# A two-layer hybrid decoder trunk on one core: the opening rebuilt, two closings and the halves of w_up moved, and 20 transposes of the identity on PE before the first tile

## The reference

```
for l in range(2):
    h = rmsnorm(x, norm_mix)
    q_a, k_a, v_a, q_b, k_b, v_b, z, xbc, dt_raw = split_cols(h @ w_in, IN_SIZES)
    q_a, k_a = apply_rope(q_a, positions), apply_rope(k_a, positions)
    y_a = swa_sink_attention(q_a, k_a, v_a, swa_sinks)        # 8 heads, window 128
    y_b = moba_attention(q_b, k_b, v_b)                       # 8 heads
    y_c = ssd_mixer(z, xbc, dt_raw, conv_w, conv_b, dt_bias, a_log, d_skip, ssd_norm)
    g_a, g_b, g_c = jnp.split(sigmoid(h @ w_gate + b_gate), 3, axis=-1)
    x = x + (g_a * (y_a @ w_br_swa) + g_b * (y_b @ w_br_moba) + g_c * (y_c @ w_br_ssd)) @ w_mix_out
    x = x + CrossAttn(rmsnorm(x, norm_cross), rmsnorm(mem, norm_mem))
    x = x + jnp.square(jax.nn.relu(rmsnorm(x, norm_mlp) @ w_up)) @ w_down
return rmsnorm(x, final_norm)
```

## Time and profile before

| what | value |
|---|---|
| median of 3 runs | 1207.43 us |
| the profiled execution's own time | 1205.99 us |
| its span | 1204.2 us |
| PE busy | 1168.9 us (97%) |
| DVE busy | 774.5 us (64%) |
| ACT busy | 573.3 us (48%) |
| POOL busy | 66.1 us (5%) |
| loads | 199.04 MB read, 166 GB/s over the span |

### The profile page before, as it was taken

One profiled execution on the slowest core, in us unless ns is written; L12 is line 12 of the kernel. 1 busy time (PEld: TensorE's weight loads), 2 busy tenths in 40 slices (PEclk: granted clock), 3 DMA queues, 4 the chain that ended last, 5 costly groups with the idle time before them and its releaser, 6 DMA issues. The chain is left out here.

```text
span 1204.2 us, 18337 instructions
## 1 busy us (share of the span) xinstructions
PE 1168.9 (97%) x7503; PEld 1047.6 (87%) x7503; DVE 774.5 (64%) x1172; ACT 573.3 (48%) x808; POOL 66.1 (5%) x93
## 2 busy tenths in 40 slices
PE   4999999999999999999999999999999999999997
PEld 3998899999998887888889888999989988888886
DVE  5877765886654456656568677568685445655655
ACT  5545454534554355344355545544455444534443
POOL 2000001410000000000000000043000000000000
PEclk9999999999999999999999999999999999999999
DMA  5743525746643445655636533366655443575560
GB/s 183 229 156 110 171 71 179 232 137 218 199 165 133 154 148 188 210 175 176 209 109 209 175 126 120 112 186 193 204 182 190 152 148 105 175 243 168 190 220 36
DMA packets 156412, 201.31 MB, mean 167 GB/s; under 512 B 7152, under 2 KB 111912, under 8 KB 156328
## 3 DMA queue, kind: packets, MB, share of 16 engines
q1 hardware_dynamic: 155296, 199.46, 51.0%
q10 hardware_dynamic: 1032, 0.67, 0.2%
HBM read 199.04 MB, written 1.08 MB: 166 GB/s over the span
## 5 line engine op out<-in xcount | busy, mean ns | idle before, releaser
L1401 DVE TENSOR_TENSOR w_lo<-raw,w_hi 128x2048 fp32r<-128x2048 f32 (+1 forms) x184 | 412.5, 2245 | 249.6 <-ACT w_hi L742 249.5
L742 ACT ACTIVATE w_hi<-raw 128x2048 fp32r<-128x2048 f32 (+1 forms) x184 | 343.2, 1875 | 108.4 <-PE psum L1114 78.5
L1097 PE MATMUL psum<-act_both,w_hi 128*128 128x256 f32 x832 | 240.9, 290 | 0.0
L1099 PE MATMUL psum<-act_both,w_lo 128*128 128x256 f32 x832 | 235.2, 283 | 0.0
L1098 PE MATMUL psum<-act_both,w_hi 128*128 128x256 f32 x832 | 235.2, 283 | 0.0
L1085 PE MATMUL psum<-act_both,w_hi 128*128 128x512 f32 x512 | 181.8, 399 | 2.3 <-DVE w_lo L1401 2.3
L1097 PEld LDWEIGHTS psum<-act_both,w_hi 128*128 128x128 f32 x832 | 159.3, 191 | 1.1 <-issue 0.5
L1098 PEld LDWEIGHTS psum<-act_both,w_hi 128*128 128x128 f32 x832 | 159.4, 192 | 0.6 <-issue 0.5
L1099 PEld LDWEIGHTS psum<-act_both,w_lo 128*128 128x128 f32 x832 | 159.2, 191 | 0.0
L1086 PE MATMUL psum<-act_both,w_lo 128*128 128x256 f32 x512 | 143.5, 280 | 0.0
L1085 PEld LDWEIGHTS psum<-act_both,w_hi 128*128 128x128 f32 x512 | 96.1, 188 | 27.2 <-DVE w_lo L1401 3.1
(11 more groups left out here) (252 smaller groups left out, 1923.9 us busy)
## 6 DMA issues: line engine op xcount, KB each, us to landing
raw<-in_w_in_dram SPq DMA_DIRECT2D x35, 1024.0 KB, 5.0
raw<-in_w_up_dram SPq DMA_DIRECT2D x32, 1024.0 KB, 5.4
raw<-in_w_down_dram SPq DMA_DIRECT2D x32, 1024.0 KB, 4.9
raw<-in_w_gate_dram SPq DMA_DIRECT2D x24, 1024.0 KB, 7.1
raw<-in_w_ckv_dram SPq DMA_DIRECT2D x16, 1024.0 KB, 5.2
raw<-in_w_br_ssd_dram SPq DMA_DIRECT2D x8, 1024.0 KB, 10.0
raw<-in_w_mix_out_dram SPq DMA_DIRECT2D x8, 1024.0 KB, 5.0
raw<-in_w_cq_dram SPq DMA_DIRECT2D x8, 1024.0 KB, 5.3
```

The source lines that it names most:

```text
L742: act.activation(w_hi[:, slot, 0:n], raw[:, slot, 0:n], ACT.Copy).then_inc(hi_ready.sem, 1)
L1097: pe.matmul(dst, m_hi[:, k, cs], a_hi[:, k, :], start=k == 0, stop=False)
L1099: ins = pe.matmul(dst, m_lo[:, k, cs], a_hi[:, k, :], start=False, stop=k == kt - 1)
L1401: dve.tensor_tensor(w_lo[:, slot, 0:n], raw[:, slot, 0:n], w_hi[:, slot, 0:n].bitcast(F32), ALU.subtract).then_inc(lo_ready.sem, 1)
```

## The change

**Opening, layer 0.** SP loads both x tiles first, then units 0 and 1 in halves, unit 2, the seven parameter rows (moved from ACT's queue), the four parameters by heads, unit 3. ACT issues three loads, squares two values of a constant (`mark_act`), squares both x tiles, and then splits units 0 and 1 by halves, with a bank of activations between any two (`hi_half`, `norm_gain_hi`). DVE scales both tiles, and alternates `lo_half` and `norm_gain_lo` likewise; the rope angles (`sine_angles`) move behind unit 3's `lo`. PE makes each half unit of a tile in blocks: all hi x hi, then hi x lo, then lo x hi (`opening`), in the order (unit, tile) = (0,0), (0,1), (1,0), (1,1); `rows_turn` stands before the last. Ahead of it all PE makes 20 transposes of the identity into bank 3, which nobody reads.

**Opening, layer 1.** The order stays (0,0), (1,0), (0,1), (1,1), in blocks as above; unit 1 is split in halves, tile 1's transposes stand around the second half of (1,0), and `norm_gain_lo` of bank 2 comes before `lo` of unit 2.

**Middle.** `ACS_SLOT` one slot later. Closing 1 one slot later. Closing 6 from behind unit 33 into the middle of unit 34. `yoff` from YB to SB. `xs_tokens` reads tile 1 first.

**w_up.** `relu_hi` moves behind the split of unit u+3 (`relu_high`); the third norm's squares move to slot U_UP+4 and write their waste to `xdec`.

The diff, cut to its core:

```
-ACS_SLOT, BTOK_SLOT, CB_SLOT, STATES_SLOT = U_XBC[3] + 1, U_XBC[4] + 3, U_XBC[5] + 4, U_XBC[5] + 6
+ACS_SLOT, BTOK_SLOT, CB_SLOT, STATES_SLOT = U_XBC[3] + 2, U_XBC[4] + 3, U_XBC[5] + 4, U_XBC[5] + 6
-TURN_SLOT = [s + (2 if i < 3 else 1) for i, s in enumerate(CLOSE_SLOT)]
+INNER_CLOSINGS, OUTER_CLOSINGS = (0, 1, 2, 6), (3, 4, 5, 7)
+TURN_SLOT = [s + (3 if i == 1 else 2 if i in INNER_CLOSINGS else 1) for i, s in enumerate(CLOSE_SLOT)]
...
         if branch == 2 and tile == 1 and s == CLOSE_SLOT[i]:
-            out.append((YB_, ("yoff", group)))
+            out.append((SB_, ("yoff", group)))
...
                     if l == 0 and u == RING:
+                        for name, r0, n in (("norm_cross", 8, 8), ("norm_mem", 16, 8), ("norm_mlp", 24, 8),
+                                            ("ssd_norm", PC_SSDN, 8), ("conv_b", PC_CONVB, 12),
+                                            ("b_gate", PC_BGATE, 24)):
+                            sp.dma_start(rows[r0:r0 + n, :, :], a[name].rearrange("l (k p) -> k l p", p=P))\
+                              .then_inc(par_loaded, 16)
...
+                    if (l, u) == (0, 0):
+                        for t in range(TT):
+                            sp.dma_start(x_sb[:, t, :], a["x"][0, t * P:(t + 1) * P, :]).then_inc(x_loaded[t], 16)
+                    if l == 0 and u < 2:
+                        sp.dma_start(dst[:, 0:2, :], src[:, 0:2, w["col"]:w["col"] + n])\
+                          .then_inc((raw_first, raw_second)[u], 16)
...
+            act.wait_ge(lo_ready.sem, RING)
+            act.activation(mark_act[:], pool_c[:, 0, :], ACT.Square)
...
                     ins.then_inc(up_lo.sem, 1)
-                    act.wait_ge(*relu_sq.at(l, j + 1))
-                    act.activation(relu_hi[:, (j // 2) % 2, 2 * (j % 2):2 * (j % 2) + 2, :], two(pT_sb[:, j % 2, :]),
-                                   ACT.Copy).then_inc(relu_h.sem, 1)
                     return
...
                     if u + RING < NU and w["kind"] != "xbc":
                         hi(l, u + RING)
+                    if (l, u) == (0, U_QA + 1):
+                        sines()
+                    if w["kind"] == "up":
+                        relu_high(l, w["index"])
...
-                    if u == NORM_TURN_SLOT[2] or u == U_CO + 3:
+                    if u == NORM_TURN_SLOT[2] or u == U_UP + 4:
...
+            for _ in range(20):
+                pe.transpose(psum[:, 3, 0:P], ident[:], ident[:])
...
+            def opening(l, u, t):
...
+                pe.wait_ge(*norm_hi.at(l, 2 * t + u + 1))
+                for ks in ((0, 1), (2, 3)) if t == 0 else (range(4),):
...
+                    for k in ks:
+                        pe.matmul(dst, act_hi[:, 4 * u + k, ts], m_hi[:, k, :], start=u == 0 and k == 0, stop=False)
+                    if last:
+                        wait_lo(pe, l, u)
+                    else:
+                        pe.wait_ge(*(lo_first, lo_second)[u].at(l, 1))
+                    for k in ks:
+                        pe.matmul(dst, act_hi[:, 4 * u + k, ts], m_lo[:, k, :], start=False, stop=False)
+                    pe.wait_ge(*is_read(l, ("norm", 0, 2 * t + u)))
+                    for k in ks:
+                        ins = pe.matmul(dst, act_lo[:, 4 * u + k, ts], m_hi[:, k, :], start=False,
+                                        stop=u == 1 and k == 3)
+                    if (u, t) == (l > 0, 0) and not last:
+                        norm0_turn(l, 1, (0,))
+                if (u, t) == (l > 0, 0):
+                    norm0_turn(l, 1, (1,))
...
                         if (l, u) == (0, 2):
-                            pe.wait_ge(cols_ready, 1)
+                            pe.wait_ge(cols_turned, 2)
...
-                for t in range(TT):
+                for t in (1, 0):
                     key = ("xs", g, t)
```

More of the change, by code:

```diff
@@ L833, in evacuate, with relu_high @@
                     ins.then_inc(free((u, 0)), 1)
+            def relu_high(l, j):
+                act.wait_ge(*relu_sq.at(l, j + 1))
+                act.activation(relu_hi[:, (j // 2) % 2, 2 * (j % 2):2 * (j % 2) + 2, :], two(pT_sb[:, j % 2, :]),
+                               ACT.Copy).then_inc(relu_h.sem, 1)
             def merged_hi(l, j):
@@ L907, in start @@
                 square(0, 0, x_sb, sq_done.sem)
-                act.wait_ge(*unit_done.at(l, prev_user(0) + 1))
                 if l == 0:
[L910 to L915, removed]
+                    x_left(act, l, 1)
@@ L916, in start @@
+                    square(0, 1, x_sb, sq_done.sem)
+                hi_half(l, 0, 0)
                 if l == 0:
                     act.wait_ge(mix_cols, 1)
[L918 to L932, removed]
+                    norm_gain_hi(l, 0, (0,))
+                    hi_half(l, 0, 1)
+                    norm_gain_hi(l, 0, (1,))
+                    hi_half(l, 1, 0)
@@ new lines, in sines @@
+            def sines():
+                act.wait_ge(angle_ready, 1)
+                act.activation(cos2[:, :, 0:32], angles[:, 0], ACT.Sin).then_inc(sines_ready, 1)
+                act.activation(sin2[:, :, 32:64], angles[:, 1], ACT.Sin).then_inc(sines_ready, 1)
+                act.wait_ge(cols_turned, 2)
+                act.wait_ge(cols_ready, 1)
+                act.activation(half[:], cols[:, :, 0:PC_ROWS], ACT.Copy, scale=0.5).then_inc(half_ready, 1)
+                act.wait_ge(half_ready, 1)
+                act.wait_ge(heads_loaded, 16 * 4)
@@ L1312, in _ @@
                     if u in GROUPS:
-                        if u == U_QA and l == 0:
-                            norm0_turn(l, 0)
+                        if u == U_QA:
+                            if l == 0:
+                                norm0_turn(l, 0)
+                            for i, t in ((0, 0), (0, 1), (1, 0), (1, 1)) if l == 0 else ((0, 0), (1, 0), (0, 1), (1, 1)):
+                                if (l, i, t) == (0, 1, 1):
+                                    rows_turn()
+                                opening(l, i, t)
+                            continue
                         for t in range(TT):
@@ L1529, in scaled, with lo_half @@
                        .then_inc(htok_done.sem, 1)
-                if l:
+                def lo_half(u, part):
+                    cs = slice(1024 * part, 1024 * (part + 1))
+                    if part:
+                        dve.wait_ge(*hi_ready.at(l, u + 1))
+                    else:
+                        dve.wait_ge(*(hi_first, hi_second)[u].at(l, 1))
+                    made = lo_first if u == 0 else (lo_second, lo_ready)[part]
+                    dve.tensor_tensor(w_lo[:, u, cs], raw[:, u, cs], w_hi[:, u, cs].bitcast(F32), ALU.subtract)\
+                       .then_inc(made.sem, 1)
@@ L1533, in start @@
                         down_out(l - 1, 0, j)
[L1534 to L1541 removed]
+                    scaled(0)
@@ L1587, in evacuate @@
                     return
+                if (l, kind) == (0, "qa"):
+                    parameters()
                 dve.wait_ge(*unit_done.at(l, u + 1))
```

204 lines of the change are left out of this document (118 added, 86 removed).

## The result

| | before | after |
|---|---|---|
| median of the runs | 1207.18 us (4 runs, 1206.81 to 1207.82) | 1189.30 us (4 runs, 1188.45 to 1191.27) |
| ratio | | 0.9855, interval 0.9841 to 0.9870 |
| the profiled execution, its span | 1205.99 us, 1204.2 us | 1189.82 us, 1188.1 us |

The change makes the kernel 17.9 us (1.5%) faster; the forecast was 1187.3, within 1182.5 to 1192.5. Profile against profile it is 16.2 us, not 17.9, where the sum had 20.1; why the three differ is taken up at the end.

The account below looks back on a forecast made before the run. PE, busy 97% of the span, bounds the kernel, so only its waits can be won. Eight terms sum to 20.1 us: 1205.99 becomes 1185.9, plus 1.44 from profile to median gives 1187.3 us, range 1182.5 to 1192.5.

Parts of the forecast that it names:

- The opening, -9.3: Opening of layer 0: earlier loads, squares and scaling let unit 2 start at 22.9 in place of 32.2 us.
- the sign of being wrong: Unit 2 after 27, or a PE wait of over 2 us in a place not among the earlier profile's waits.
- The 20 transposes: Ahead of the opening: with 8 transposes they raise the clock, products 0.23 apart from the first; own cost nothing.
- rival 1: In the opening the transposes don't raise the clock: +2.4, 1189.7 us; chance 0.26.
- A wait of 1.74 did not lower the clock: Before closing 6: transposes behind that wait took 0.66 against 0.60, so some 2 us before the first product wouldn't either.
- w_up, -4.1: Up units: with the split ahead of relu_hi, waits for w_lo (2.3) and relu_lo (1.8) go; bounds 0 and 4.6.
- Closing 1, -2.0: Closing 1: one slot later DVE is not behind a convolution, winning 2.0 of a 2.2 us wait.
- Rivals 2 and 4: 2: opening's feeders late, up to +3, 1190.3, chance 0.12; 4: relu_hi behind a split awaiting a load, slower, 0.03.
- Closing 6, -1.5: Closing 6's 3.8 us wait goes, but PE waits again at closing 7; only 0.75 counts, twice; bounds 0 and 3.8.
- xs, -0.7: SSD values: tile 1 first frees bank 4, but the next turn waits for tile 0 in bank 7; 0.7 of 0.9.
- Layer 1's opening, -1.0: Unit 1's w_lo in halves comes 1.1 sooner, but PE then meets tile 1's h_tok; bounds 0 and 1.5.
- The first product behind a wait, -0.8: It takes longer (0.77 against 0.62); some six waits fewer, each 0.13; between nothing and 1.5.

Follow-up runs that it names:

- Run 5: The kernel before with all of the change but the openings of both layers and the transposes: 1198.93 us, ratio 0.9921.
- run 8: The changed kernel with closing 1 one slot sooner again, in unit 18: 1192.27 us, 2.2 over the changed kernel.
- run 3: The changed kernel with 18 more transposes of the identity behind the 8 of tile 0, filling PE's wait: 1187.76 us, 2.3 under the changed kernel.
- run 2: The changed kernel without the 20 transposes of the identity: 1191.42 us, 1.3 slower than the changed kernel.
- the 37 runs: The kernel before, unchanged, run 37 times beside the experiments: 1204.97 to 1211.01 us, mean clocks 0.995 to 0.999.
- run 4: The kernel before with only the 20 transposes added behind PE's first transpose: 1205.71 us against 1207.54 beside it, ratio 0.9986.
- run 7: The changed kernel with closing 6 turned behind unit 33 again, y_off still in bank 4: 1192.29 us, 2.2 over the changed kernel.
- run 1: The changed kernel measured again, nothing altered: 1190.08 us, ratio to before 0.9847.
- run 9: The changed kernel with relu_high back ahead of ACT's split of unit u+3, squares staying at slot U_UP+4: 1194.69 us, 4.6 over.
- run 6: The changed kernel with the rope angles ahead of the first tile's scaling on DVE again: 1194.59 us, 4.5 over the changed kernel.
- run 10: The changed kernel with 18 more transposes behind tile 0's, and SSD values tile 1 first only for group 0: 1186.39 us, 1.4 under run 3.

## Why the prediction was right, and where it was not

The mechanism was right: PE's waits bound the kernel, and most parts of the change were worth about the waits that they removed. That the median came within 2.0 us of the forecast is in part luck, since the sum was 3.9 too large for the profiled execution and the step from profile to median gave 2.0 back.

- **What bounds the kernel: right.** Run 5 and the undone parts each change the time by PE's waits at one place, give or take the clock. (The seven groups of the earlier trace rows sum to 12.8 us, not 12.0; no term rests on the total.)
- **The opening, -9.3: 7.75 in the profile.** The chain of arrivals held within 0.1 to 1 us: scale, h_tok, the first product, DVE's alternation. What failed is the sentence that a wait of some 2 us before the first product leaves the clock up. It did in run 8's profile and did not in the profiles of the changed kernel. There it cost 1.16 of the 1.55 missing (run 3); the rest is spread over the blocks. The sign named for it, starts 0.23 apart from the first product, was not met. And the sign of being wrong, a wait of over 2 us outside, was met to the letter by the 2.24 that the forecast itself expected: it was badly drawn.
- **The 20 transposes: half of each case.** They raise the clock, as the forecast took it, against rival 1; but what they give is mostly lost in the wait of 2.24. In medians they are worth 1.3 us as they stand and 3.7 with the wait filled (run 2 against run 3). In the opening itself the traces show 0.2 and 1.4 (24.64 against 24.42 and 23.26), where rival 1 had put 2.4: without them the low stretch ends after some seven products and four transposes, not twelve products.
- **"A wait of 1.74 did not lower the clock": the step that was wrong in kind.** It was one place of one execution. At closing 6 in other profiles waits of 1.76, 1.87 and 1.99 did, at up to 1.4 us each, and waits of 1.92 and 2.02 did not. The prediction also added the 1.44 between profile and median to its sum as if it stayed. By the mean clocks of the 37 runs, the profile of before was of an execution that kept its clock behind the opening and the median of one that lost some; that the loss stood at closing 6 fits runs 4 and 7, but the slower runs of before themselves have no profile that shows it. The median after is 0.5 under its profile, and 0.1 in run 1.
- **w_up, -4.1: right,** 4.6 in run 9. **Closing 1, -2.0: right,** 2.2. **acs (the sum of a_dt), -0.7: right,** the wait for decay is gone. **Rope angles hidden: right** (run 6). Rivals 2 and 4 did not show: the profile lists no wait of PE between its first product and unit 5, and no w_hi among the up units waited for a load.
- **Closing 6, -1.5.** The forecast saw that the wait moves on to closing 7, though not because DVE has no idle time there: the earlier trace rows has 0.95 of it, for POOL. It did not see the next station, the first mix unit, bound by loads queued behind closing 7's y_tok. Waits alone give it little (3.9 for y_tok against 2.3 and 1.0), and the measured 2.2 is mostly the clock.
- **xs, -0.7: wrong.** The term looked at the bank that is freed sooner and said only that the next turn waits for bank 7. For group 1 that is all there is: 1.4 us lost to it (run 10), and the total of the group went from 0.9 to 1.1.
- **Layer 1's opening, -1.0: right.** From tile 0's transposes to unit 2 it takes 16.88 in place of 17.87. Its waits for w_lo and issue went, and one of 1.2 for h_tok stands in their place, as forecast.
- **The first product behind a wait, -0.8: not isolated.** Among the w_up units the first start is 0.34 from the next in place of 0.23, so each wait fewer is worth some 0.1 beyond its length, an estimate, and behind the opening 7 waits of over 0.3 are left of 14.
- **All behind the opening: 10.8 forecast, 8.4 in the profile.** The waits for xd_sb, which the forecast had gone, and for act_both, which it did not have, 2.1 us in all, make up most of what is missing.

## What to carry to other kernels

Follow a wait that is removed through two more stations of the waiting engine, not one, and look at each engine and queue that sets them. Dummy work that raises the clock pays reliably only if nothing behind it lets PE stand again: fill up to the first real product. And a wait of some 2 us on PE may cost nearly twice its length in part of the executions, so a single profile in which it did not is no bound.

## What the runs showed of the hardware

- Waits of 1.76 (run 4), 1.87 and 1.99 (run 7), 1.90 (run 1), 2.13 (run 7), 2.24 (the profile after) and 2.33 us (run 9) on PE were followed by a granted clock of 1.2 GHz; waits of 1.74 and 2.02 (before), 1.92 (run 4), 2.01 (run 2) and 2.43 (run 8) were not. The low stretch cost 1.2 us in the opening and 1.4 in the middle.
- Transposes of a 128x128 identity in float32 raise the clock and hold it: 20 took 4.53 us in the profile after, about 0.22 each as at the low level, and the 8 behind them 1.10; in run 3 the 18 behind those took 2.13.
- The granted clock of the windows can't be trusted ahead of its first rise. In run 2 it reads 1.00 from 7 to 13 us, where 8 transposes took 1.97 and pairs of products 1.05; the distance of starts tells the level there.
